# Expert weights loaded in pairs of tiles, with the down weights issued by ScalarE

## The reference, cut to what matters

```python
def swiglu(h, w_in, w_out):
    a, b = jnp.split(h @ w_in, 2, axis=-1)
    return (jax.nn.silu(a) * b) @ w_out

# moe_swiglu: FF_EXPERT = 3584, D = 1024, float32
for e in range(8):
    y = y + gates[:, e:e + 1] * swiglu(hf, w_in[e], w_out[e])   # w_in[e]: 1024 x 7168, w_out[e]: 3584 x 1024
```

## Time and profile before

| what | value |
|---|---|
| median of 3 runs | 1502.25 us (1496.95 to 1505.79) |
| the profiled execution | 1499.91 us |
| its span | 1498.2 us |
| TensorE busy | 1448.5 us, 97% of the span |
| DMA moved | 501.73 MB, 335 GB/s over the span |
| expert stage | 601.0 us to about 1482 us of the span |

### The profile page before, as it was taken

One profiled execution on the slowest core, in us unless ns is written; L12 is line 12 of the kernel. 1 busy time (PEld: TensorE's weight loads), 2 busy tenths in 40 slices (PEclk: granted clock), 3 DMA queues, 4 the chain that ended last, 5 costly groups with the idle time before them and its releaser, 6 DMA issues.

```text
span 1498.2 us, 24011 instructions
## 1 busy us (share of the span) xinstructions
PE 1448.5 (97%) x9451; PEld 796.3 (53%) x9451; DVE 606.5 (40%) x988; ACT 395.4 (26%) x597; POOL 65.3 (4%) x48
## 2 busy tenths in 40 slices
PE   5999999999999999999999999999999999999996
PEld 2788877888878977333333333333333333333332
DVE  1888999888888886100012010210001210011013
ACT  3635544534446664200111011000011010100001
POOL 0222210000000011000000000000000000000000
PEclk8999999999999999999999999999999999999998
DMA  9987768788884547799999999999999999999993
GB/s 331 346 282 254 290 225 281 265 297 307 308 298 170 206 169 257 271 381 398 399 396 399 397 395 399 396 397 399 395 397 398 395 395 396 396 397 396 396 398 123
DMA packets 224418, 501.73 MB, mean 335 GB/s; under 512 B 13328, under 2 KB 44224, under 8 KB 209984
## 3 DMA queue, kind: packets, MB, share of 16 engines
q1 hardware_dynamic: 223152, 500.31, 89.9%
q10 hardware_dynamic: 1168, 0.07, 0.0%
HBM read 499.28 MB, written 1.05 MB: 334 GB/s over the span
## 4 chain that ended last, share of the span: by engine, by line
PE 65%; SPq 10%; DVE 10%; DMA 9%; issue 4%; ACT 1%; DVEq 0%; ACTq 0%
PE ps L1163 20%; PE ps L1187 10%; SPq L508 8%; PE ps L1172 7%; PE ps L625 4%; DMA ada<-in_ada_w 4%; PE ps L627 4%; PE ps L626 4%; PE ps L1196 3%; DVE acc L1850 3%; DVE w_lo L1831 3%; DMA raw<-in_moe_w_out 2%; DMA w_whole<-in_moe_w_out 2%; PE ps L1207 2%; SPq L516 1%
## 5 line engine op out<-in xcount | busy, mean ns | idle before, releaser
L1831 DVE TENSOR_TENSOR w_lo<-raw,w_hi 128x1024 fp32r<-128x1024 f32 x162 | 204.9, 1273 | 8.2 <-ACT w_hi L1411 7.6
L2310 DVE TENSOR_TENSOR FA<-ps,FA 128x256 f32<-128x256 f32 x56 | 23.8, 425 | 408.1 <-ACT FA L1760 408.1
L1411 ACT ACTIVATE w_hi<-raw 128x1024 fp32r<-128x1024 f32 x162 | 165.6, 1053 | 66.6 <-PE ps L627 52.0
L1163 PE MATMUL ps<-raw,FA 128*64 128x512 f32 x784 | 177.8, 597 | 1.4 <-issue 1.1
L1163 PE MATMUL ps<-w_whole,FA 128*64 128x512 f32 x768 | 174.7, 598 | 0.0
L1754 ACT ACTIVATE FA<-ps 128x512 f32<-128x512 f32 x56 | 33.4, 597 | 421.9 <-PE ps L1172 312.3
L625 PE MATMUL ps<-w_hi,hT_hi 128*128 128x512 f32 x352 | 140.5, 399 | 0.8 <-DVE w_lo L1831 0.5
L1850 DVE SCALAR_TENSOR_TENSOR acc<-ada,cond,acc 128x512 f32<-128x512 f32 x168 | 138.6, 825 | 3.0 <-DMA ada<-in_ada_w 1.0
L627 PE MATMUL ps<-w_hi,hT_lo 128*128 128x512 f32 x352 | 138.2, 393 | 0.0
L626 PE MATMUL ps<-w_lo,hT_hi 128*128 128x512 f32 x352 | 137.2, 390 | 0.0
L2303 DVE COPY FA<-ps 128x256 f32<-128x256 f32 x35 | 14.8, 423 | 262.0 <-PE ps L1172 262.0
(11 more groups left out here) (344 smaller groups left out, 1758.5 us busy)
## 6 DMA issues: line engine op xcount, KB each, us to landing
raw<-in_moe_w_in SPq DMA_DIRECT2D x196, 512.0 KB
w_whole<-in_moe_w_in SPq DMA_DIRECT2D x192, 512.0 KB
w_whole<-in_moe_w_out SPq DMA_DIRECT2D x48, 1024.0 KB
ada<-in_ada_w SPq DMA_DIRECT2D x46, 1024.0 KB, 7.3
raw<-in_moe_w_out SPq DMA_DIRECT2D x46, 1024.0 KB
ada<-in_moe_w_in SPq DMA_DIRECT2D x60, 512.0 KB
raw<-in_ff_w_in SPq DMA_DIRECT2D x44, 512.0 KB
ada<-in_moe_w_out SPq DMA_DIRECT2D x18, 1024.0 KB
```

The costliest lines, as they stand in the source:

```text
L1163: last = pe.matmul(ps[64 * g:64 * g + 64, Z, :], h[:, kc, 0:CAP], w[k // 2][:, k % 2, g, :], start=kc == 0, stop=kc == KC - 1)
L1411: act.activation(w_hi[:, cn % RING, cols], raw[:, cn % RAW, cols], ACT.Copy).then_inc(hi_done, 1)
L1831: v.tensor_tensor(w_lo[:, cn % RING, cols], raw[:, cn % RAW, cols], w_hi[:, cn % RING, cols].bitcast(f32), ALU.subtract).then_inc(lo_done, 1)
```

## The change

The work is cut into 32 **items** instead of 56 units. Each expert has four: three pairs of tiles and one single. A pair's up weights are loaded 1024 columns wide, eight slots with row pieces of 4 KB, two DMAs per slot; a single keeps the old 2 KB layout. `ITEM`, `width`, `parts` and `tile_no` replace `UNIT` and its counts; the order table is written anew in items, and the ring order stays up(n+1), down(n), up(n+2).

TensorE's `up(n, i)` runs the 64-row matmuls of tile 0, then of tile 1, over the same four slots, and then the overflow of both tiles at once (512 columns instead of 256). `step` runs both halves of up, then `down(n-1)` of tile 0, then waits for the copies out of PSUM (`summed`), runs `between`, transposes z of tile 0, runs `down(n-1)` of tile 1, and transposes z of tile 1. Gathers, scatters and transposes all move to the `between` behind the first down. `down` waits for both of its slots before its first matmul.

`load_down` moves from SyncE to ScalarE and stands at the end of ScalarE's `step(n)`, behind both silus and, in the FOLD steps, behind `y_high`. SyncE issues the up weights alone.

Not shown: the renamed counts, the PSUM banks (`Z` is now banks 0 and 1, `ZO` is bank 7), second buffers for `zs` and `e32`, `fnorm`'s new place in FA, and VectorE's step, which does the same operations per tile.

```diff
+FEW_AT = (2, 4, 7, 9, 12, 14, 17, 19, 22, 24, 26, 28)
+FULL_AT = tuple(n for n in range(ITEMS) if n not in FEW_AT)
+ITEM = {n: (True, j // 4, j % 4) for j, n in enumerate(FEW_AT)} | {n: (False, j // 4, j % 4) for j, n in enumerate(FULL_AT)}
+TURN_HOT = {2: 0, 8: 1, 15: 2, 23: 3, 29: 4}
+TURN_FEW = {5: 0, 13: 1, 25: 2}
+PICK = {2: 1, 8: 2, 15: 3, 23: 4}
+PICK_FEW = {5: 1, 13: 2}
+GATHER = {3: 1, 10: 2, 16: 3, 25: 4}
+ROWS = {4: 1, 11: 2, 17: 3, 26: 4}
+GATHER_FEW = {0: 0, 8: 1, 19: 2}
+ROWS_FEW = {1: 0, 9: 1, 20: 2}
+FOLD = {6: 0, 12: 1, 19: 2, 26: 3}
+FOLD_FEW = {10: 0, 22: 1, 29: 2}
+BLOCK = ((0, 1), (6, 7))
+SCATTER = {7: 0, 14: 1, 22: 2, 28: 3}
+SCATTER_FEW = {12: 0, 24: 1}
+SCATTER_LAST = {30: 0, 31: 1}
...
+    return 1 if ITEM[n][2] == 3 else 2
...
 def up_slot(n):
-    return max(6 * n - 2, 0)
+    return 4 * units_to(n) + 2 * units_to(max(n - 1, 0))
 
 
 def down_slot(n):
-    return 6 * n + 8 if n < UNITS - 1 else MOE_U - 2
+
+    return 4 * units_to(min(n + 2, ITEMS)) + 2 * units_to(n)
...
+                u = 2 * ITEM[n][2]
+                if width(n) == 2:
+                    for k in range(KC):
+                        r = up_slot(n) + k
+                        freed(r, p)
+                        for g in range(2):
+                            sp.dma_start(moe_raw(r)[:, g * D:(g + 1) * D],
+                                         w_ab[ds(e * D + k * P, P), ds(g * FE + u * TW, 2 * TW)]).then_inc(m_in[r % SLOTS], 16)
+                    return
...
-            def load_down(n, p, e):
-                u = UNIT[n][2]
-                for h in range(2):
-                    r = down_slot(n) + h
-                    freed(r, p)
-                    sp.dma_start(moe_raw(r).rearrange("p (t n) -> p t n", t=2),
-                                 w_dn[ds(e * FE + (u * TW + h * 2 * P), 2 * P), :].rearrange("(p t) n -> p t n", t=2))\
-                      .then_inc(m_in[r % SLOTS], 32)
...
+                for j in parts(n):
+                    if n == 0 and i == 0 and j == 1:
+                        rows_there(0, p)
+                    for kc in range(4 * i, 4 * i + 4):
+                        if j == parts(n)[0] and (wide or kc % 2 == 0):
+                            arrived(r + (kc if wide else kc // 2), p)
+                        w = of_tile(n, r, j, kc)
+                        for g in range(2):
+                            last = pe.matmul(ps[64 * g:64 * g + 64, Z[j], :], h[:, kc, 0:CAP], w[:, g, :], start=kc == 0,
+                                             stop=kc == KC - 1)
+                        if few and j == 1 and (wide or kc % 2):
+                            last.then_inc(raw_gone, 1)
...
+                if not few and quarters_first:
+                    rows_32()
...
+            def summed(n, p):
+
+
+                pe.wait_ge(esa_ok, tile_no(n, 1, p))
+                if not ITEM[n][0]:
+                    pe.wait_ge(eg_ok, full_no(n, 1, p))
+
             def step(n, p):
 
                 rows_there(n, p)
                 up(n, p, 0)
+                up(n, p, 1)
+                first_down(n - 1, p)
+                pair = width(n - 1) == 2
+                pe.wait_ge(eTl_ok, tile_no(n - 1, parts(n - 1)[0], p))
+                if pair:
+                    down(n - 1, p, 0, range(4), not ITEM[n][0])
+                else:
+                    down(n - 1, p, 1, range(2))
+                summed(n, p)
+                pe.wait_ge(eTl_ok, tile_no(n - 1, 1, p))
                 between(n, p)
-                up(n, p, 1)
-                second_block(n, p)
-                if n in GATHER_FEW:
-                    pe.wait_ge(f_ht_ok, NW * p + (GATHER_FEW[n] + 1))
-                    transpose_gathered(CAPF, f_hgT_done)
-                if n in TURN_HOT:
-                    hot_gone(n, p)
-                    transpose_hot(hot, CAPF, hotT_done)
-                if n in TURN_FEW:
-                    hot_gone(n, p)
-                    transpose_hot(f_hot, CAPF, f_hotT_done)
-                pe.wait_ge(eTl_ok, UNITS * p + n)
-                first_down(n - 1, p)
-                down(n - 1, p)
+                if width(n) == 2:
+                    transpose_z(n, p, 0)
+                if pair:
+                    down(n - 1, p, 1, range(4))
+                else:
+                    down(n - 1, p, 1, range(2, 4))
+                if width(n) == 2:
+                    pe.wait_ge(eTl_ok, tile_no(n, 0, p))
+                transpose_z(n, p, 1)
...
             def z_out(n, p):
-                act.wait_ge(raw_gone, gone(up_slot(n) + 4, p))
-                act.activation(in_rows(zs[:, 0, :]), by_chunk(ps[:, Z, :]), ACT.Copy).then_inc(esa_ok, 1)
+                act.wait_ge(raw_gone, gone(up_slot(n) + 4 * width(n), p))
+                for j in parts(n):
+                    act.activation(in_rows(zs[j]), by_chunk(ps[:, Z[j], :]), ACT.Copy).then_inc(esa_ok, 1)
...
+            def load_down(n, p, e):
+
+                u = 2 * ITEM[n][2]
+                for h in range(2 * width(n)):
+                    r = down_slot(n) + h
+                    act.wait_ge(raw_gone, gone(r - SLOTS + 1, p))
+                    act.dma_start(moe_raw(r).rearrange("p (t n) -> p t n", t=2),
+                                  w_dn[ds(e * FE + (u * TW + h * 2 * P), 2 * P), :].rearrange("(p t) n -> p t n", t=2))\
+                       .then_inc(m_in[r % SLOTS], 32)
...
+                        full = act.value_load(ids[0:1, turn:turn + 1], min_val=0, max_val=NE - 1)
                     step(n, p)
+                    load_down(n, p, few if is_few else full)
```

More of the change, by code:

```diff
@@ L51 @@
 assert TURNS * SLOTS == MOE_U
[L54 to L61, removed]
@@ L85, in gone, with tile_no, full_no @@
     return r + MOE_U * p
[L88 to L94, removed]
+def tile_no(n, j, p):
+    return units_to(n) + j - (2 - width(n)) + 1 + UNITS * p
+def full_no(n, j, p):
+    return full_units_to(n) + j - (2 - width(n)) + 1 + NF * ET * p
 def by_chunk(z):
@@ L525, in experts @@
                 load_up(0, p, full)
[L526 to L528 removed]
+                for n in range(1, ITEMS):
+                    is_few, turn, u = ITEM[n]
                     if n == FEW_AT[0]:
@@ L1157, in up @@
[L1157 to L1166, removed]
+                r, wide = up_slot(n), width(n) == 2
@@ L1176, in up, with down @@
                         last.then_inc(raw_gone, 1)
-            def down(n, p):
-                few, _, u = UNIT[n]
-                r = down_slot(n)
+            def down(n, p, j, chunks, quarters_first=False):
+                few, _, u = ITEM[n]
+                r = down_slot(n) + 2 * (j - parts(n)[0])
+                first, final = u == 0 and j == 0, u == 3
                 w = [moe_raw(r + h).rearrange("p (t n) -> p t n", t=2) for h in range(2)]
-                for c in range(4):
+                for c in chunks:
@@ L1184, in down @@
                     if c % 2 == 0:
                         arrived(r + c // 2, p)
[L1186 to L1191, removed]
@@ L1192, in down, with rows_64 @@
-                if few:
-                    return
-                for c in range(4):
[L1195 to L1207, removed]
+                def rows_64():
+                    for c in chunks:
+                        for g in range(2):
+                            last = pe.matmul(ps[64 * g:64 * g + 64, YW if few else Y, :], e32[j][:, c, 0:CAP],
+                                             w[c // 2][:, c % 2, g * TW:(g + 1) * TW], start=first and c == 0,
+                                             stop=final and c == 3)
+                        if c % 2 and (few or quarters_first):
+                            last.then_inc(raw_gone, 1)
@@ new lines, in rows_32 @@
+                def rows_32():
+                    for c in chunks:
+                        for q in range(4):
+                            last = pe.matmul(ps[32 * q:32 * q + 32, YO, 0:S], e32[j][:, c, CAP:CAPF],
+                                             w[c // 2][:, c % 2, q * S:(q + 1) * S], start=first and c == 0,
+                                             stop=final and c == 3)
+                        if c % 2 and not quarters_first:
+                            last.then_inc(raw_gone, 1)
@@ L1792, in _ @@
                     first_rows(p)
-                z_out(0, p)
-                gate_silu(0, p)
-                for n in range(1, UNITS):
+                full, few = FIRST, None
+                for n in range(ITEMS):
+                    if n == FEW_AT[0]:
+                        act.wait_ge(id_ok, 1)
+                    is_few, turn, u = ITEM[n]
+                    if u == 0 and is_few:
+                        few = act.value_load(ids[0:1, NF + turn:NF + turn + 1], min_val=0, max_val=NE - 1)
+                    elif u == 0 and n:
+                        full = act.value_load(ids[0:1, turn:turn + 1], min_val=0, max_val=NE - 1)
                     step(n, p)
+                    load_down(n, p, few if is_few else full)
```

(4 more changed lines are left out.)

218 lines of the change are left out of this document (123 added, 95 removed).

## The result

The changed kernel takes 1548.9 us (median of 4, 1537.4 to 1552.9) against 1503.8 us (median of 4): the ratio is 1.030, 95% interval 1.026 to 1.034. It is slower, as forecast, but by some 45 us and not by 10: outside the forecast's range, which ended at 1538.

What follows compares the result with a forecast made beforehand. It took TensorE as the bound, with the DMA a hair behind. 1499.9 - 14.4 - 3.9 + 2.2 + 6.7 + 20 = 1510.5 us, so about 1512 us in the median's scale; range 1487 to 1538, the forecast's own 1502 to 1530.

Steps and rivals of the forecast that it cites:

- What bounds: Expert stage: TensorE sets the time at 874.4 us, about 9 us of it not work, with the DMA a hair behind.
- part 1: TensorE's matmuls change shape 234 times instead of 330, at 0.15 us each: 14.4 us off.
- its 853 us: DMA bound of the old expert stage: 352.3 MB at 396 GB/s, less the 14 slots in the ring at the start.
- The sum without the move: Expert stage with the shape, DMA-wait and first-item terms, but without the costs of moving the down loads: 858.3 us.
- Part 2: 4 KB pieces for up weights: rate near 402 to 407 GB/s, removing 3.9 us of TensorE's waits and no more.
- Part 3: First item, with nothing to cover its waits for copies, silu and product: +2.2 us.
- Part 4: Down loads issued late, at ScalarE's end of step: +20 us at seven places, other steps covered except the last.
- the landing of a group: Late down loads, taking two thirds of the stream: two slots there after 9.5 us, four after 17.1 us.
- The deduction of 0.8 us at each of seven places: SyncE has only about two slots queued at the start of each place; this lowers 25.7 us to 20 us.
- The last down: Last step, down load issued after the last transposes without cover: 7.9 us instead of 1.2, +6.7 us.
- The rival of half rate: Late down loads get half rate or less, and a ring runs dry: 1530 to 1560 us, chance 17%.
- Its other half: The ring runs dry, so that TensorE waits for up weights too; part of the 17% rival.

Runs made afterwards that it cites:

- experiment 5: Changed kernel with down loads back on SyncE in ring order, and a pair's up weights in 2 KB instead of 4 KB pieces: 1514.1 us, ratio 1.009.
- 6 and 7: Two variants of the changed kernel: down loads as two DMAs of 4 KB pieces, 1603.1 us; separately, a pair's up weights in 2 KB pieces, 1562.2 us.
- Experiment 4: Changed kernel with TensorE doing unused identity matmuls during the waits at seven steps and before the last down: 1546.8 us, ratio 1.025.
- experiment 2: Changed kernel with down loads still on ScalarE, but issued as soon as their slots are free: 1502.0 us, ratio 0.998.
- experiment 3: Kernel before (units of one tile, 2 KB pieces) with only the down loads moved to the end of ScalarE's step: 1578.1 us, ratio 1.049.
- down_4k: Changed kernel with each down load split into two DMAs with 4 KB instead of 8 KB pieces: 1603.1 us, one run.

## Why the prediction was wrong in size

- **What bounds, and part 1.** Part 1 was right. Counted in the traces, the changes of shape fall from 330 to 234 as forecast. TensorE's busy time in the stage falls from 869.3 to 857.5 us with SyncE's order, of which 3.4 are slow matmuls, so by 15.2 us without them, where 14.4 were forecast; no run changes the shapes alone. The 512-wide overflow takes 3.57 us with its change of shape, twice 1.72 and 0.15. What bounds was half right. Idle time in the stage before was 5.1 us, not about 9. But from 650 us on its stream was full as well (1.04, 397 GB/s), and its bound had left out the slow start, so the DMA was nearer than its 853 us say.
- **The sum without the move.** It had 874.4 - 14.4 - 3.9 + 2.2 = 858.3 us for the stage, and 865.3 were measured: 9.1 us saved and not 16.1. By the medians that variant lies 16.2 us under before, which fits the 16.1 by luck. What lies between is in its trace: a wait of 2.25 us with 1.7 of slow matmuls behind it, 1.3 more than forecast in the first item and 1.7 of slow matmuls behind that, and 1.0 at one pair's second transposes (item 20, 1165.82), less the 0.8 by which part 1 was low.
- **Part 2** had the rate nearly right (405 on average forecast, 410 measured) but its worth wrong: "removes the 3.9 us of waits and no more". It is worth 19 us in the stage of pairs, because with coarse items and 2 KB pieces the stream and not TensorE would set the time (experiment 5). The two errors, ends of the stream not priced and rate not priced, nearly cancel in the changed kernel.
- **Part 3**: forecast +2.2, which with the 0.72 of before are 2.9 us of waits; seen 1.38 before the first item's `between` and 2.87 before its second transposes, 4.25. Small and too low. The second wait was priced by the last unit's silu and product, and the first silu has a table load in front of it, which before lay beside matmuls:

```profile
634.45 1.28 ACT L1820 ACT_TABLE_LOAD   x1
635.75 0.38 ACT L1820 ACTIVATE FA<-ps 128x256 f32<-128x256 f32 x1
```
- **Part 4 failed, and this is the step that made the miss.** Its mechanism and its places were right: 5, 7, 9, 11, 18, 25 and 28 were named and all waited; item 19, taken as covered, waited too (1.80). Its size was 20 us; measured are 34.4 us of waits. The term that was mis-sized is the landing of a group: 9.5 us for two slots and 17.1 for four were put in, 12.2 to 12.6 (13.5 at item 25) and 20.3 to 21.0 came out. It has two parts, estimated in 6 and 7: down gets some 55% of the stream and not two thirds, and the start takes 2.6 us and not 2.0. Part 4's own rules with 12.4 and 20.6 us in place of 9.5 and 17.1 give some 50 us at the seven places, as an estimate; measured there are 32.3 of waits and 14.7 of slow matmuls, most of which stand where there would be more waiting at full speed. The deduction of 0.8 us at each of seven places, for SyncE's short queue, was wrong as well.
- **The clock wasn't in the sum at all.** In the stage each wait of 2.5 us and more was followed by matmuls that took 1.7 to 2.6 us longer: 14.7 us in seven places at down, 1.7 in the first item, and 2.4 at the last down. Experiment 4 shows that mostly these hid under the landing of the next slots: removing the seven gave 6.0 us at their items and 3.5 in the whole stage, and 0.8 behind it. Before has no wait over 1.2 us in the stage, so it says nothing of what a longer one does. The Trainium skill's page "TensorE: Matmul & The Clock Gate" (HAM oscillation — how this bites in real kernels) describes a clock that falls in a wait for DMA, so that the matmuls behind it run slow; the trace after agrees, with 0.50 at 892 to 896 us.
- **The last down** was right: forecast +6.7, seen 7.66 - 1.20 = +6.5, and 8 us by the ratios with its slow stretch. Its 0.9 us for the issue stood on no row; in the trace after, the two issues run from 1519.76 to 1520.66.
- **The rival of half rate** (17%) came out: its price of 1530 to 1560 holds the time, and its sign, a four-slot load over 18 us, was seen. Its other half didn't come: up weights were waited for once (0.34 us).
- Together: against the variant with SyncE's order, the move costs 47.1 us in the stage and 8.9 behind it (6.4 of wait, 2.4 of clock), 56 us; by the medians 59. Forecast were 26.7.
- A second queue's price was not in the sum either: issued early enough from ScalarE, the down loads still cost 12 us against SyncE's one order (experiment 2). The Trainium skill's page "DMA: Bandwidth & Descriptors" (Issuing engines are not separate DMA queues) has it that a second issuing engine shares the same DMA engines and relieves only the issue; the runs agree: over 50 us the stream reached 414 GB/s at most, with two queues as with one.

## What to carry to other kernels

A load that is issued at the end of a step is covered only by what the consumer does before it asks, so price it by the shortest such stretch, with the landing time under a shared stream and not alone; four slots of 1 MiB took 20 us and not 10. Keep the loads of one ring in one queue in the order in which they are used; a second queue cost 12 us here even with early issue. When two resources are both full, test a faster transfer in its place before calling it worthless.

## What the runs showed of the hardware

- Two queues shared the DMA engines unevenly by piece size: ScalarE's had some 45, 55 and 63% for pieces of 4:4, 8:4 and 8:2 KB (estimates, one place each).
- One queue's stream: 387 GB/s in 2 KB pieces, 397 in a mix of 2 and 8 KB, 410 in a mix of 4 and 8 KB.
- In the stage of the changed kernel TensorE's granted clock fell behind every wait of 2.5 us and more (to 0.50 at 892 to 896 us), and not behind waits of 1.67 and 1.80. Other runs don't keep to that length: it fell behind 1.97 and 1.99 us (experiment 4), and stayed at 1.00 behind 2.03 (experiment 3) and 2.83 (down_4k, at 1303.63).
- The table load before ScalarE's first silu took 1.28 us.
